# An encoder trunk on one core: attention's values projected with tokens on the partitions, and another order of the projection tiles

## The reference, cut to what matters

```python
u = _rmsnorm(h, mix_norm[l])
p = u @ w_in[l]                                   # 3584 columns = 28 tiles of 128
rq, rk, rv, rg, dq, dk, dv = jnp.split(p, splits, axis=-1)
ret = _retention(rq, rk, rv, rg, ret_decay_logit[l], ret_gn_g[l])
dif = _diff_attn(dq, dk, dv, diff_qn_g[l], diff_kn_g[l], diff_lambda[l], diff_subln_g[l],
                 rel_bias_table, lam_init)
h = h + jnp.concatenate([ret, dif], axis=-1) @ w_out[l]
```

## Time and profile before

| | |
|---|---|
| median of 3 runs | 1937.66 us (1937.4 to 1937.69) |
| the profiled execution's own time | 1936.88 us |
| its span, first to last instruction | 1934.8 us |
| granted TensorE clock, mean | 0.992 |
| PE, PEld, POOL, DVE, ACT busy | 98%, 87%, 62%, 60%, 47% |
| attention of layer 0 on PE | 371.24 to 596.68 us: 225.4 us |
| attention of layer 1 on PE | 1324.2 to 1549.6 us: 225.4 us |

### The profile page before, as it was taken

The page is one execution under the profiler, slowest core; times in us unless marked ns, Lnnn a source line. Parts: engine busy times, 40 slices in busy tenths (PEclk is TensorE's granted clock), DMA queues, the critical chain, the costliest instruction groups (busy, mean ns, idle before and its releaser), DMA issues.

```text
span 1934.8 us, 29797 instructions
## 1 busy us (share of the span) xinstructions
PE 1895.0 (98%) x11578; PEld 1689.3 (87%) x11578; DVE 1154.2 (60%) x1881; ACT 916.2 (47%) x1461; POOL 1202.8 (62%) x810
## 2 busy tenths in 40 slices
PE   8999999999999999999989999999999999999997
PEld 7989989887888898989879899998778889899896
DVE  6636657437755653726667376563576466367276
ACT  6435535456425543524565254454564265345254
POOL 4857858464444676857558586765545267578582
PEclk9999999999999999999999999999999999999999
DMA  4333323232223132332224223223221132323231
GB/s 142 125 109 110 131 90 110 80 98 66 72 70 109 67 131 71 105 109 91 85 95 146 88 94 125 88 88 107 79 66 66 55 109 89 120 98 121 77 107 68
DMA packets 54999, 186.46 MB, mean 96 GB/s; under 512 B 6440, under 2 KB 7976, under 8 KB 54860
## 3 DMA queue, kind: packets, MB, share of 16 engines
q1 hardware_dynamic: 53136, 181.61, 28.0%
q10 hardware_dynamic: 1724, 2.96, 0.4%
HBM read 182.44 MB, written 3.15 MB: 96 GB/s over the span
## 4 chain that ended last, share of the span: by engine, by line
PE 85%; POOL 5%; DVE 4%; ACT 3%; issue 1%; DMA 1%; SPq 0%; ACTq 0%; DVEq 0%; POOLq 0%
PE bank L673 17%; PE bank L675 17%; PE bank L674 17%; PE pair L673 8%; PE pair L675 8%; PE pair L674 8%; POOL w_lo L585 2%; PE pair L923 1%; PE pair L951 1%; PE bank L908 1%; PE bank L963 1%; DMA raw<-in_w_gu 1%; PE bank L713 1%; PE bank L722 1%; PE bank L717 1%
## 5 line engine op out<-in xcount | busy, mean ns | idle before, releaser
L576 POOL TENSOR_TENSOR w_lo<-raw,w_hi 128x512 fp32r<-128x512 f32 (+1 forms) x248 | 324.5, 1333 | 400.1 <-ACT w_hi L1030 399.9
L673 PE MATMUL bank<-hg_hi,w_hi 128*128 128x256 f32 (+1 forms) x1400 | 451.0, 322 | 0.5 <-POOL w_lo L585 0.3
L674 PE MATMUL bank<-hg_lo,w_hi 128*128 128x256 f32 (+1 forms) x1400 | 445.0, 318 | 0.0
L675 PE MATMUL bank<-hg_hi,w_lo 128*128 128x256 f32 (+1 forms) x1400 | 444.8, 318 | 0.0
L673 PEld LDWEIGHTS bank<-hg_hi,w_hi 128*128 128x128 f32 x1400 | 268.0, 191 | 22.1 <-issue 4.4
L674 PEld LDWEIGHTS bank<-hg_lo,w_hi 128*128 128x128 f32 x1400 | 268.2, 192 | 18.4 <-issue 1.2
L675 PEld LDWEIGHTS bank<-hg_hi,w_lo 128*128 128x128 f32 x1400 | 267.9, 191 | 17.8
L1030 ACT ACTIVATE w_hi<-raw 128x1024 fp32r<-128x1024 f32 (+1 forms) x124 | 128.6, 1037 | 266.2 <-PE bank L675 128.7
L1439 DVE SCALAR_TENSOR_TENSOR h<-pair,h 128x512 f32<-128x512 f32 x100 | 68.9, 690 | 249.9 <-PE pair L675 249.7
L673 PE MATMUL pair<-a_hi,w_hi 128*128 128x512 f32 x440 | 172.7, 393 | 1.9 <-issue 1.0
L675 PE MATMUL pair<-a_hi,w_lo 128*128 128x512 f32 x440 | 171.7, 390 | 0.0
(11 more groups left out here) (265 smaller groups left out, 4910.3 us busy)
## 6 DMA issues: line engine op xcount, KB each, us to landing
raw<-in_w_gu SPq DMA_DIRECT2D x96, 512.0 KB, 3.7
raw_x<-in_w_gu SPq DMA_DIRECT2D x80, 512.0 KB, 4.0
raw<-in_w_p SPq DMA_DIRECT2D x56, 512.0 KB, 3.4
raw_x<-in_w_dn SPq DMA_DIRECT2D x32, 512.0 KB, 3.7
raw<-in_w_dn SPq DMA_DIRECT2D x32, 512.0 KB, 3.6
raw<-in_w_o SPq DMA_DIRECT2D x16, 512.0 KB, 3.5
raw_x<-in_w_dn SPq DMA_DIRECT2D x16, 384.0 KB, 3.4
raw<-in_w_dn SPq DMA_DIRECT2D x16, 384.0 KB, 3.4
```

Of the source, the lines that this page charges most:

```text
L576: ins = pool.tensor_tensor(columns(lo_[:, part, :]), source[:, part.start * P:part.stop * P], columns(hi[:, part, :]).bitcast(F32), ALU.su ...
L673: pe.matmul(out, hi[:, 0, :], m_hi, start=first, stop=False)
L674: pe.matmul(out, hi[:, 0, :], m_lo, start=False, stop=False)
L675: return pe.matmul(out, lo_[:, 0, :], m_hi, start=False, stop=last)
```

## The change

The values are projected the other way round: the input (128 tokens of it) is the stationary operand and the weights of two heads, 256 columns in two slots, are the moving one. The result has tokens on the partitions and needs no turning. A pair of value tiles still takes two steps: the first makes tokens 0 to 255 (two groups of 24 matmuls), the second tokens 256 to 511. Because both steps read both slots, nothing is split after the first and two units are split after the second; the first also needs both units ready. The norm factor is now one number a partition, `token_rms`, made once by VectorE from the diagonal of `rms`. ScalarE takes the values out of their banks with it (`take_values`); for retention it also sums each token's 128 features, and VectorE subtracts the mean (`centre_values`) in the step after, behind that step's `take_over`. The constant `centre` goes.

```diff
+TILES = [("rg", h) for h in range(HEADS)]
+for _h in (0, 2):
+    TILES += [("dv", _h), ("dv", _h + 1)] + [(k, h) for h in (_h, _h + 1) for k in ("dk", "dq")]
+TILES += ([("rv", 0), ("rv", 1)] + [(k, h) for h in range(3) for k in ("rk", "rq")]
+          + [("rv", 2), ("rv", 3), ("rk", 3), ("rq", 3)])
...
-def scores_at(n): return 7 + 3 * (n // 2) + n % 2
+def scores_at(n): return (9, 10, 11, 12, 15, 16, 18, 19)[n]
...
-def ret_scores_at(h): return 19 + 3 * h
+def ret_scores_at(h): return (21, 23, 25, 28)[h]
...
+                        if second_value(t):
+                            lo(l, E_ATT + AHEAD + t - 1)
+                        if not first_value(t):
+                            lo(l, E_ATT + AHEAD + t)
...
+            def value_product(l, t):
+
+                s = t % SLOTS // 2 * 2
+                for tt in (0, 1) if first_value(t) else (2, 3):
+                    out = proj[t][:, (tt % 2) * SEQ:(tt % 2 + 1) * SEQ].rearrange("p (a b) -> p a b", a=2)
+                    tokens = slice(tt * P, (tt + 1) * P)
+                    for k in range(KD):
+                        hi, lo_ = w_hi[:, s:s + 2, k, :], w_lo[:, s:s + 2, k, :]
+                        pe.matmul(out, hg_hi[:, k, tokens], hi, start=k == 0, stop=False)
+                        pe.matmul(out, hg_lo[:, k, tokens], hi, start=False, stop=False)
+                        last = pe.matmul(out, hg_hi[:, k, tokens], lo_, start=False, stop=k == KD - 1)
+                return last
...
-                        pe.wait_ge(value_free, at(value_free, l, VALUES.index(("rv", hd_n)) + 1))
+                        pe.wait_ge(value_centred, at(value_centred, l, hd_n // 2 * 2 + 2))
+                        if hd_n:
+                            pe.wait_ge(o_ret_free, at(o_ret_free, l, hd_n))
...
+            def take_values(l, t):
+
+                kind, hd = TILES[t][0], TILES[t - t % 2][1]
+                if t == VALUES[0]:
+                    act.wait_ge(token_ready, at(token_ready, l, 1))
+                if kind == "rv":
+
+                    act.wait_ge(mixv_done, at(mixv_done, l, 2 * hd + 4))
...
+                for tt in (0, 1) if first_value(t) else (2, 3):
...
+                        ins = act.activation(flat(v[:, tt, hd:hd + 2, :]), proj[t][:, at_:at_ + SEQ], ACT.Copy, scale=scale)
...
+                        for j in range(2):
+                            i = 2 * (tt % 2) + j
+                            ins = act.activation(v[:, tt, hd + j, :], proj[t][:, at_ + j * P:at_ + (j + 1) * P], ACT.Copy,
+                                                 scale=scale, accum_out=value_sum[:, i:i + 1])
+                ins.then_inc(value_taken, 1)
...
-                    if t < PROJ_TILES:
+                    if t < PROJ_TILES and t not in VALUES:
                         take_over(l, t)
+                    if t - 1 in VALUES and TILES[t - 1][0] == "rv":
+                        centre_values(l, t - 1)
                     if t == 1:
...
+                        dve.tensor_tensor(diagonal, rms[:, :].rearrange("p (a b) -> p a b", b=P), spread, ALU.mult)\
+                            .then_inc(token_diag, 1)
+                        dve.wait_ge(token_diag, at(token_diag, l, 1))
+                        dve.tensor_reduce(token_rms[:, :], diagonal, AX.X, ALU.add).then_inc(token_ready, 1)
...
+            def centre_values(l, t):
+
+                hd, tt = TILES[t - t % 2][1], 2 * (t % 2)
+                dve.wait_ge(value_taken, at(value_taken, l, VALUES.index(t) + 1))
+                base = value_sum[:, :]
+                spread = bass.AP(base.tensor, base.offset, [list(base.ap[0]), [2, 2], [1, 2], [0, P]])
+                values = v[:, tt:tt + 2, hd:hd + 2, :]
+                dve.scalar_tensor_tensor(out=values, in0=spread, scalar=-1.0 / P, in1=values, op0=ALU.mult, op1=ALU.add)\
+                    .then_inc(value_centred, 1)
```

More of the change, by code:

```diff
@@ L117, with first_value, second_value @@
         _count[_r] += 1
-TILES = ([("rg", h) for h in range(HEADS)] + [(k, h) for h in range(HEADS) for k in ("dk", "dq", "dv")]
-         + [(k, h) for h in range(HEADS) for k in ("rk", "rq", "rv")])
+TILES = [("rg", h) for h in range(HEADS)]
[3 more added lines that the diff above has]
+          + [("rv", 2), ("rv", 3), ("rk", 3), ("rq", 3)])
+VALUES = [t for t, tile in enumerate(TILES) if tile[0] in ("dv", "rv")]
+assert all(TILES[t][1] % 2 == t % 2 for t in VALUES)
+def first_value(t):
+    return t in VALUES and t % 2 == 0
+def second_value(t):
+    return t in VALUES and t % 2 == 1
 COLUMN = {"rq": 0, "rk": 4, "rv": 8, "rg": 12, "dq": 16, "dk": 20, "dv": 24}
@@ L148 @@
 PAIRS = []
-VALUES = [tile for tile in TILES if tile[0] in ("dv", "rv")]
 for _t in range(STEPS):
@@ L474, in stat_index, with taken @@
             return order.index((which, i))
+        def taken(l, t):
+            if t in VALUES:
+                return value_taken, at(value_taken, l, VALUES.index(t) + 1)
+            return proj_free, at(proj_free, l, sum(i not in VALUES for i in range(t + 1)))
         block = ctx.enter_context(nc.Block())
@@ L877, in attention @@
                         s = t % SLOTS
-                        pe.wait_ge(lo_done, at(lo_done, l, E_ATT + t + 1))
+                        pe.wait_ge(lo_done, at(lo_done, l, E_ATT + t + 1 + first_value(t)))
                         if t >= 3:
-                            pe.wait_ge(proj_free, at(proj_free, l, t - 2 if t < 5 else t - 1))
-                        last = product(proj[t], s, hg_hi, hg_lo, KD)
+                            pe.wait_ge(*taken(l, t - 3 if t < 5 else t - 2))
+                        if t in VALUES:
+                            last = value_product(l, t)
+                        else:
+                            last = product(proj[t], s, hg_hi, hg_lo, KD)
                         last.then_inc(proj_done, 1)
@@ L925, in attention @@
                         last.then_inc(pair_done, 1)
[L926 to L943, removed]
                     if (hd_n := at_step(ret_scores_at, HEADS, t)) is not None:
@@ L1306, in attention @@
                         act.wait_ge(proj_done, at(proj_done, l, t + 1))
-                        split(l, E_ATT + AHEAD + t)
+                        if second_value(t):
+                            split(l, E_ATT + AHEAD + t - 1)
+                        if not first_value(t):
+                            split(l, E_ATT + AHEAD + t)
+                        if t in VALUES:
+                            take_values(l, t)
                     if kind == "rg":
-                        act.wait_ge(proj_free, at(proj_free, l, t + 1))
+                        act.wait_ge(*taken(l, t))
                         act.activation(rg[:, hd, :], rg[:, hd, :], ACT.Silu).then_inc(rg_ready, 1)
```

47 lines of the change are left out of this document (24 added, 23 removed).

## The result

The changed kernel takes 1951.34 us (median of 4 runs, 1950.47 to 1952.13), the kernel before 1937.68 us on the same chips (4 runs, 1937.4 to 1937.91): ratio 1.007, 95% interval 1.0053 to 1.0088. It is slower by 13.7 us, where 11.2 were forecast. The profiled execution took 1950.98 us, its span is 1949.2 us, and the mean granted clock fell from 0.992 to 0.988.

The account below looks back on a forecast made before the run. TensorE, working 98% of the span, was taken to bound the kernel. Per layer -5.4 + (1.6 + 2.2 + 1.0 + 4.4) + 1.8 = +5.6 us, two layers +11.2: 1948.9 us, range 1939 to 1959.

Parts of the forecast that it names:

- four places: New TensorE waits forecast per layer at steps 7, 19, 21 and 26: 1.6, 2.2, 1.0 and 4.4 us.
- TensorE's own work: Per layer: 5.20 us of turning and centring removed, 0.3 given back, 2.2 added by narrower value matmuls; sum -2.7 us.
- The rival of loads that are not hidden: Doubled weight loads of value tiles exposed on TensorE: 56 us, 1994 us without new waits; chance 0.01.
- The old stall: TensorE's 2.69 us idle at the statistic of step 14, taken as gone: -2.7 us a layer.
- Step 7: Statistic of dk 0 waits for load, split, square, low part and low square: 1.6 us (1.3 to 1.9).
- Step 19: Turn of item 5 waits for VectorE's list in step 18: 2.2 us, between 0.4 and 3.0.
- Step 21: Turn of item 6 waits because VectorE is still behind: 1.0 us, between 0 and 3.0.
- Step 26: Weighted sum of head 2 waits for the last centring, queued behind a take-over: 4.4 us, between 3.8 and 4.8.
- The clock: Granted clock falls behind the idle of step 26: +1.8 us a layer (1.4 to 2.2); other waits 0.
- hidden waits: Waits at steps 19 and 21 absent, clock does not fall: 0 a layer, 1937.7 us; chance 0.12.
- VectorE keeps up: Waits at steps 19, 21 and 26 and the clock loss vanish: -3.8 us a layer, 1930.1 us; chance 0.08.
- Worse contention: Old 2.7 us stall stays, clock falls again at step 19: +10.1 us a layer, 1957.9 us; chance 0.11.

Follow-up runs that it names:

- the kernel before without its turning: Kernel before, its value-tile transpositions and centring products left out, values copied unturned, output not the reference's: 1930.01 us, ratio 0.9958.
- the fifth experiment: Changed kernel with each centring in VectorE's list of its tile's own step, ahead of the retention head output: 1934.43 us, ratio 0.9981 to the kernel before.
- centring in its step and squares first: Changed kernel with each centring in its tile's own step and GpSimd's low square ahead of the low weights in every q and k step: 1931.04 us, ratio 0.9964.
- The second experiment: Changed kernel with GpSimd making the low part of the square ahead of that of the weights in steps 6 and 12: 1949.9 us, ratio 1.0063.
- the filler: Changed kernel with 18 unused 512-column matmuls ahead of the wait of step 26 in both layers: 1948.54 us, ratio 1.0055 to the kernel before.
- The swap experiment: Changed kernel with VectorE centring the previous tile's values ahead of the step's take-over instead of behind it: 1937.65 us, ratio 0.9999 to the kernel before.
- the two reorderings that were tried: Differential head outputs behind weights and scores: all of them, against the changed kernel, 1954.01 us; only head 1's, with own-step centring and low squares first, 1931.99 us.
- the run with the head outputs later: Changed kernel with VectorE making each differential head's output behind the softmax weights and scores of its step: 1954.01 us, ratio 1.0084 to the kernel before.

## Why the prediction was right

The sign, the mechanism and its four places were right, and 1951.3 us lies 2.4 above the 1948.9 forecast, inside both ranges. Part of that closeness is luck: the misses on single waits cancel. Step by step:

- **TensorE's own work, -2.7 a layer: too much by 0.8.** The kernel before needs 225.42 - 2.69 = 222.7 us a layer without its idle time. The changed kernel needs 220.8 in both layers without its idle time and without the clock's loss (below): -1.9. The 5.20 us of turning are real (the kernel before without its turning), and the value pace is 11.40/95 = 0.120 us (404.62 less 393.22, with 95 intervals), 5.76 us a tile, +0.32 instead of +0.27. Most of the rest is that a wait costs more than its recorded idle time, since the product ahead of it ends later than the next matmul could have started: product 26 takes 5.64 us up to its recorded end, and 5.49 to the next start in the fifth experiment, where no wait follows. The prediction counted these 0.16 us inside its waits, and the recorded waits leave them out. With the wait of step 26 gone (the fifth experiment) the work is 220.6 us, and with that of step 7 gone too (centring in its step and squares first) 222.7 - 2.48 = 220.2, so -2.5. The rival of loads that are not hidden is refuted: each of those matmuls has a load of its own. By the rule on loads that stood beside it, of the page "TensorE: Matmul & The Clock Gate" of the Trainium skill ("What overlaps and what doesn't"), they would have been exposed; the measurement decides against it for these full-array matmuls.
- **The old stall gone, -2.7: right** in both layers.
- **Step 7, +1.6: right on the mean**, with 2.06 and 1.10 us both outside the stated 1.3 to 1.9. The load in the chain was put at 3.69 us; from the end of the first unit's low part to ScalarE's next split it took 4.30 us in the first layer and 3.34 in the second, which is the whole difference. The second experiment removed the wait by its cause.
- **Step 19, +2.2: right**, 2.06 twice. The list was the named one, with two of its instructions at 1.78 and 1.77 us where the undisturbed row has 0.75.
- **Step 21, +1.0: right in the first layer**, 0.98, and 0.24 in the second. The wait is 0.24 us in every layer of these traces in which the clock fell behind step 19 with the same order of work (the changed kernel's second, both of squares first, the filler's second), and 0.98 where it did not: a slower TensorE comes later to the same weights. So 0.74 us of that fall's cost are given back here.
- **Step 26, +4.4: right**, 4.79 twice, at the upper bound: 0.2 us from the product's end until VectorE starts, then its queue from 563.53 to 568.01, and 0.1 to the start. The swap experiment shows that the place in the queue is the cause, and the centring itself took 0.68 us where GpSimd was at rest. The Trainium skill's page "SBUF — State Buffer" ("SBUF: two separate sides") has VectorE and GpSimd lock a port pair for a whole instruction; the rows 1.75 beside 564.48 + 2.98 and 0.68 without agree.
- **The four waits together** are 9.9 and 8.2 us, mean 9.0 (9.2 with the 0.17); the forecast sum was 9.2. Step 26 came 0.4 longer than forecast, step 21 on the mean 0.4 shorter and step 19 0.1.
- **The clock, +1.8 a layer "(the others are shorter, 0)": mis-sized, too little by 1.0.** Its loss can be read by setting equal work of the changed kernel beside that of the fifth experiment, where the clock did not fall in the attention. From the weighted sum of step 26 to the next statistic, then from the weighted sum behind the turn of step 19 to the next product (second layer), in the changed kernel and below it in the fifth experiment:

```profile
577.81 0.39 PE L772 MATMUL bank<-a_hi,ones_r 128*128 128x512 f32 x1
...
1538.05 0.39 PE L772 MATMUL bank<-a_hi,ones_r 128*128 128x512 f32 x1
...
1467.35 1.85 PE L946 MATMUL bank<-a_t,v 128*128 128x256 f32 x4
...
1471.01 0.50 PE L695 MATMUL bank<-hg_hi,w_hi 128*128 128x512 f32 x1
```

```profile
561.91 1.89 PE L985 MATMUL bank<-s,v 128*128 128x256 f32 x8
...
569.09 0.39 PE L772 MATMUL bank<-a_hi,ones_r 128*128 128x512 f32 x1
...
1458.10 1.03 PE L946 MATMUL bank<-a_t,v 128*128 128x256 f32 x4
...
1460.13 0.50 PE L695 MATMUL bank<-hg_hi,w_hi 128*128 128x512 f32 x1
```

Behind step 26 that is 9.70 us (568.11 to 577.81) and 8.72 (1529.33 to 1538.05) against 7.18 in both layers, a loss of 2.5 and 1.5 us; behind step 19 3.66 against 2.03, a loss of 1.6 us, in the second layer alone. Together 2.5 us in the first layer and 3.2 in the second. So the prediction had two things too small: the one stretch of the first layer cost more than the 1.4 to 2.1 us read from the earlier trace rows, and the 2.06 us wait of step 19 was put at nothing because 2.69 us had left the clock alone.

With these sizes the sum closes: in the first layer -1.9 of work, +7.37 of waiting (10.06 - 2.69) and the clock's 2.5 give 7.98; in the second -1.9, +5.67 and 3.2 give 6.93. Work is what is left over in each, and comes out alike in both.

Of the rivals, "hidden waits" needed a short step 19 and a steady clock, and had neither. "VectorE keeps up" forecast 1930.1 us with the wait of step 7 left and those of 19 and 21 gone. The best version removes the first, keeps the others, and takes 1931.0, so that the numbers agree by chance. "Worse contention" had its second fall of the clock, in one layer, but not its old stall.

What stays open: why the same 2.06 us wait lowers the clock in one layer and not in the other. And the two reorderings that were tried only moved the waits of steps 19 and 21; whether less work on VectorE there would remove them was not tried.

## What to carry to other kernels

When work leaves the bounding engine, follow the queue of the engine that takes it over: here 1.9 us a layer of TensorE work were saved and 8.8 to 9.9 us of waiting (net of the old stall) and clock were bought, the largest part through one instruction of 0.7 us standing behind another that had to wait for the current product. Put an instruction whose inputs are ready ahead of those that wait for the product in flight, above all when its consumer comes directly after that product. And price a long wait as its length plus the slow stretch behind it, and where it is only some 2 us long give that stretch a chance: it came behind some of these waits and not behind others.

## What the runs showed of the hardware

- The granted clock was lowered behind idle times of 2.06 us (the changed kernel, second layer, step 19) and 2.17 us (filler experiment, step 7), and was not behind 2.69 us (the kernel before, both layers) nor behind 2.06 us in the first layer. In the run with the head outputs later it was lowered behind 2.55 us in the second layer and not behind 2.56 in the first. Idle times of 1.0 to 1.7 us inside the attention never lowered it in these runs. So the length of one idle time alone does not decide.
- One such fall cost 2.5, 1.5 and 1.6 us, read from equal work at either level (the changed kernel against the fifth experiment); a fall behind step 19 was followed by a wait of 0.24 us instead of 0.98 at step 21.
- An instruction on VectorE that GpSimd holds up ended 0.3 to 0.6 us after a GpSimd low part (568.01 and 567.46; 503.45 and 502.92; 502.84 and 502.55). It does not have to be the one that a trace of another order shows: with the centring (1.78 us) out of step 18, the cast behind it took 1.40 us instead of 0.43, and of 1.78 us taken out of the list only 0.68 came off the wait.
- A wait for several semaphores was recorded as "issue" (4.79 us), although the end of one VectorE instruction 0.1 us earlier decided it.
